# Expert gates added into a zeroed DRAM table by indirect DMAs, U remainders moved from GpSimd to VectorE

## The chip, the core and the metric

The program runs on one core of one Trainium2 chip. The metric is the device time of one execution in microseconds (us); lower is better. In the profile PE is TensorE (matmuls; PEld its weight loads), DVE is VectorE, ACT is ScalarE, POOL is GpSimd, and SP is the queue that issues the plain DMAs.

## What is computed

One decoder layer over 512 tokens of width 1024. The first half (projections, sliding-window attention and an RWKV recurrence, output projection, layer norm) is not touched but for one addition. The second half is PEER, a retrieval over 128 x 128 = 16384 single-neuron experts with rows U (1024) and V (1024):

```python
def _peer(h, wq, subkeys, U, V):
    q = (hf @ wq).reshape(T, PEER_HEADS, 2, PEER_HALF)
    s = jnp.einsum('thcd,hcnd->thcn', q, subkeys).astype(jnp.float32)
    sv, si = lax.top_k(s, PEER_TOPK)
    cand = sv[:, :, 0, :, None] + sv[:, :, 1, None, :]
    cidx = si[:, :, 0, :, None] * PEER_NKEYS + si[:, :, 1, None, :]
    fv, fpos = lax.top_k(cand.reshape(T, PEER_HEADS, PEER_TOPK * PEER_TOPK), PEER_TOPK)
    fidx = jnp.take_along_axis(cidx.reshape(T, PEER_HEADS, PEER_TOPK * PEER_TOPK), fpos, axis=-1)
    gates = jax.nn.softmax(fv, axis=-1).astype(h.dtype)
    def chunk(args):
        xc, ic, gc = args
        u = jnp.take(U, ic, axis=0)
        act = jax.nn.gelu(jnp.einsum('chkd,cd->chk', u, xc), approximate=False)
        vv = jnp.take(V, ic, axis=0)
        return jnp.einsum('chk,chkd->cd', gc * act, vv)
```

So each of 512 tokens picks 8 heads x 16 experts, and its output is the sum of gate x gelu(U row . h) x V row.

## The kernel before

The kernel has four blocks with barriers between them: projections (to about 367 us), mixing (to about 600), output projection and layer norm (to about 680), and `emit_experts`, to which all that follows belongs.

**Two ways for the tokens.** Tokens 0 to 383 (three tiles of 128, TD = 384) are computed densely: gelu(U h) for all 16384 experts is made, stored to the DRAM table `scored`, read back, multiplied by a table of gates that is zero for all but the picked experts, and multiplied by V. The last 128 tokens are computed sparsely: one indirect DMA (a gather) fetches, for pick number k of all 128 tokens, 128 rows of U (512 KB), another 128 rows of V. There are 128 picks, so 256 gathers, all issued by GpSimd (`Picked.fetch`, L1373). VectorE makes a dot product per U gather (`dot`, L1380) and a weighted sum per V gather (`add`, L1399); each is one SCALAR_TENSOR_TENSOR with both inputs in SBUF.

**The U stage.** 128 slabs of 128 experts, four to a group, so 32 groups i with slots s = 0 to 3. For every slab TensorE transposes the U rows in two halves into PSUM banks 2 and 3 (`turn`, L1295, 8 matmuls), ScalarE rounds the halves to fp32r into `uh` (`evacuate`, L1323), something subtracts to get the remainder `ul`, and TensorE makes 24 matmuls (`product`, L1315: uh with hh, uh with hl, ul with hh). On TensorE `turn` of the next slab stands ahead of `product` of this one. `turn` may write banks 2 and 3 only when the previous slab has been read out of them (`bank_out`). In groups 0 to 9 ScalarE copies the banks a second time, to `uraw` (L1330), which frees them, and GpSimd subtracts from there (`remainder`, L1338). From group 10 on VectorE subtracts out of PSUM, which frees them (`late_remainder`, L1346).

**Routing.** Groups 0 to 7 each hold one routing head: on TensorE 16 + 16 matmuls of 512 columns for the queries (L1641), then the scores (L1653) around slot 0; ScalarE hands the scores over in `SS`; VectorE finds the 16 best of 128, twice, then the 16 best of 256 sums and their expert numbers (L1854 to L1877), one head behind TensorE. Its order within a head is written out by hand.

**Gates.** After group 9 VectorE makes the softmax of all heads at once (L1884 to L1899), TensorE transposes expert numbers and gates (L1670) and ScalarE copies them out. In groups 10 to 25 (16 turns, `BLOCKS`) 96 steps spread the gates over all experts: VectorE makes one-hot matrices (`hot_step`, L1905 and L1910), TensorE multiplies them (4 matmuls a step, L1687), ScalarE copies them to `stage` (L1786), SP stores 1.5 MB a group to the table `gates` (L1535). In the same turns GpSimd fetches the picks of three columns (3 U and 3 V gathers a turn), in groups 26 to 30 of four; the rest comes in the V stage. A gather of turn t + 1 waits for the dot or the add of turn t that frees its buffer (`fetched`, L1604). TensorE and VectorE go through the groups in lockstep: DVE makes the remainders, the dots in slots 0 and 1, the adds in slots 2 and 3, in program order.

**The V stage.** 32 groups: SP loads V rows, stored scores and gates (L1538 to L1548), VectorE multiplies scores by gates and makes remainders, TensorE makes 72 matmuls a group (L1704 to L1706). Layer norm and output follow.

## Time and profile before

| what | value |
|---|---|
| time, median of 3 runs | 2102.42 us (2101.3 to 2102.5) |
| the profiled execution, its own time | 2104.01 us |
| its span, first to last instruction | 2102.3 us |
| mean granted TensorE clock | 0.964 of full |
| TensorE busy | 1918.7 us (91%) |
| VectorE busy | 1428.1 us (68%) |
| ScalarE busy | 734.1 us (35%) |
| GpSimd busy | 550.0 us (26%) |
| U stage with routing, groups 0 to 9 | about 686 to 1016 us |
| U stage, groups 10 to 25 | about 1022 to 1433 us |
| U stage, groups 26 to 31 | about 1433 to 1560 us |
| V stage | about 1560 to 2085 us |

An engine that is busy most of the time is not by that the bound: a stage is bound by the engine that never waits in it. The busy time of a matmul counts from its issue to its modelled end, and the next one is issued before that; so times of TensorE are best read as distances between start times. Times in the rows are from the start of the span.

### The profile page before, as it was taken

What the parts mean: (1) busy time and instruction counts of PE and PEld (TensorE: products, weight loads), DVE (VectorE), ACT (ScalarE), POOL (GpSimd) and SP (SyncE); (2) the same over time, 40 slices, a digit from 0 to 9 for tenths busy, and PEclk for the clock granted to TensorE, in tenths of its full rate; (3) what the DMA queues carried; (4) which work ended last, traced back from release to release, by engine and by line L of the source; (5) the groups of instructions that cost most, each with busy time, mean ns of one, the idle gap of its engine ahead of it and who ended that gap; (6) DMA issues with size and microseconds to landing.
All of it is one profiled execution on the core that took longest, in us unless ns stands there. A gap on an engine that the chain in (4) does not pass through costs nothing.

```text
span 2102.3 us, 33108 instructions
## 1 busy us (share of the span) xinstructions
PE 1918.7 (91%) x10322; PEld 1602.1 (76%) x10322; DVE 1428.1 (68%) x2902; ACT 734.1 (35%) x1305; POOL 550.0 (26%) x427
## 2 busy tenths in 40 slices
PE   2889896786967999999999999999989999999996
PEld 2343585685834687879999999999988888888885
DVE  4187435445244468687488888886758888888887
ACT  1221134343222343435444444443233333333331
POOL 3011332131100222223432233224513323233310
PEclk9999998998989999999999999999999999999998
DMA  7273100000051232434589889889979999999982
GB/s 262 98 233 127 41 1 1 0 0 0 0 201 42 90 126 96 132 99 133 206 294 299 298 296 301 296 301 336 389 281 414 368 347 359 355 353 348 355 316 79
DMA packets 244203, 434.82 MB, mean 207 GB/s; under 512 B 84578, under 2 KB 157636, under 8 KB 244164
## 3 DMA queue, kind: packets, MB, share of 16 engines
q1 hardware_dynamic: 207300, 300.12, 41.2%
q0 software_dynamic: 36864, 134.23, 17.5%
q8 instruction: 18, 0.29, 0.1%
q14 instruction: 21, 0.17, 0.0%
HBM read 379.77 MB, written 54.53 MB: 207 GB/s over the span
## 4 chain that ended last, share of the span: by engine, by line
PE 65%; DVE 1%; DMA 1%; issue 1%; ACT 0%; SPq 0%; ACTq 0%; DVEq 0%
PE bank L1315 25%; PE bank L1706 8%; PE bank L1704 8%; PE bank L1705 8%; PE bank L1641 5%; PE bank L1295 5%; PE bank L1687 4%; DMA urows<-in_peer_u 1%; PE bank L1653 1%; DVE n_stats L1118 0%; DVE wide L2008 0%; DVE wide L2006 0%; DVE wide L1127 0%; SPq L1539 0%; SPq L1543 0%
## 5 line engine op out<-in xcount | busy, mean ns | idle before, releaser
L1315 PE MATMUL bank<-hh,uh 128*128 128x384 f32 x1024 | 358.3, 350 | 0.0
L1315 PE MATMUL bank<-hl,uh 128*128 128x384 f32 x1024 | 344.4, 336 | 0.0
L1704 PE MATMUL bank<-vh,wh 128*128 128x512 f32 x768 | 299.4, 390 | 3.1 <-DVE wl L1967 3.1
L1706 PE MATMUL bank<-vh,wl 128*128 128x512 f32 x768 | 299.5, 390 | 0.0
L1705 PE MATMUL bank<-vl,wh 128*128 128x512 f32 x768 | 299.4, 390 | 0.0
L1373 POOL DMA_INDIRECT vsel<-in_peer_v,picks x128 | 151.7, 1185 | 413.0 <-DVE gt L1399 398.7
L1800 ACT ACTIVATE vh<-vraw 128x1024 fp32r<-128x1024 f32 x128 | 135.9, 1062 | 288.4 <-PE bank L1706 270.2
L1373 POOL DMA_INDIRECT usel<-in_peer_u,picks x108 | 147.9, 1369 | 247.9 <-DVE usel L1380 234.6
L1964 DVE TENSOR_TENSOR vl<-vraw,vh 128x1024 fp32r<-128x1024 f32 x128 | 156.6, 1223 | 81.1 <-ACT vh L1800 81.0
L1315 PE MATMUL bank<-hh,ul 128*128 128x384 f32 x1024 | 198.3, 334 | 0.0
L1315 PEld LDWEIGHTS bank<-hl,uh 128*128 128x128 f32 x1024 | 194.4, 190 | 0.0
L1315 PEld LDWEIGHTS bank<-hh,uh 128*128 128x128 f32 x1024 | 194.2, 190 | 0.0
L1315 PEld LDWEIGHTS bank<-hh,ul 128*128 128x128 f32 x1024 | 179.3, 188 | 0.0
L1399 DVE SCALAR_TENSOR_TENSOR gt<-vsel,wsel,gt 128x1024 f32<-128x1024 f32 x128 | 164.1, 1282 | 12.7 <-DMA vsel<-in_peer_v,picks 5.2
L1704 PEld LDWEIGHTS bank<-vh,wh 128*128 128x128 f32 x768 | 144.6, 188 | 33.5 <-DVE vl L1964 3.5
L1346 DVE TENSOR_TENSOR ul<-bank,uh 128x512 fp32r<-128x512 f32 x174 | 112.0, 685 | 84.0 <-ACT uh L1323 84.0
L1705 PEld LDWEIGHTS bank<-vl,wh 128*128 128x128 f32 x768 | 144.6, 188 | 30.0
L1706 PEld LDWEIGHTS bank<-vh,wl 128*128 128x128 f32 x768 | 144.5, 188 | 30.0
L1338 POOL TENSOR_TENSOR ul<-uraw,uh 128x1024 fp32r<-128x1024 f32 x41 | 100.5, 2452 | 234.4 <-ACT uraw L1330 234.4
L464 PE MATMUL bank<-hT,wt 128*128 128x512 f32 x320 | 147.5, 619 | 9.9 <-DMA wt<-in_w_in 5.7
L1323 ACT ACTIVATE uh<-bank 128x512 fp32r<-128x512 f32 x256 | 145.1, 606 | 12.9 <-PE bank L1295 12.5
L1295 PE MATMUL bank<-ident,urows 128*128 128x128 f32 x1024 | 135.8, 276 | 13.0 <-DMA urows<-in_peer_u 6.4
(314 smaller groups left out, 3096.3 us busy)
## 6 DMA issues: line engine op xcount, KB each, us to landing
urows<-in_peer_u SPq DMA_DIRECT2D x128, 512.0 KB
vraw<-in_peer_v SPq DMA_DIRECT2D x128, 512.0 KB
ada<-in_ada_w SPq DMA_DIRECT2D x12, 2048.0 KB
scored<-act_out SPq DMA_DIRECT2D x128, 192.0 KB
gates<-SS SPq DMA_DIRECT2D x16, 1536.0 KB
gtile<-gates SPq DMA_DIRECT2D x32, 768.0 KB
act_in<-scored SPq DMA_DIRECT2D x128, 192.0 KB
wt<-in_w_in SPq DMA_DIRECT2D x19, 512.0 KB
```

The lines of the kernel that those rows point to most:

```text
L464: last = pe.matmul(banks[slot][:, :], wt[slot][:, k, :], hT[:, k, :], start=(k == 0), stop=(k == KD - 1))
L1295: last = pe.transpose(self.banks[2 + h][:, k * P:(k + 1) * P], self.u[s][:, (4 * h + k) * P:(4 * h + k + 1) * P], self.ident[:, :])
L1315: last = pe.matmul(bank, u[:, k, :], h[:, k, :], start=(n == 0), stop=(n == 3 * KD - 1))
L1323: act.activation(self.uh[s % 2][:, 4 * h:4 * h + 4, :], self.banks[2 + h][:, :].rearrange("p (k e) -> p k e", k=4), ACT.Copy)\
L1346: dve.tensor_tensor(self.ul[s % 2][:, 4 * h:4 * h + 4, :], self.banks[2 + h][:, :].rearrange("p (k e) -> p k e", k=4), self.uh[s % 2][:, 4 ...
L1373: pool.indirect_dma_start(out=into[:, :], out_offset=None, in_=row, in_offset=bass.IndirectOffsetOnAxis(ap=self.picks[:, at:at + 1], axis=0))\
L1399: dve.scalar_tensor_tensor(out=self.y[:, :], in0=self.vsel[k][:, :], scalar=self.wsel[:, k:k + 1], in1=self.y[:, :], op0=ALU.mult, op1=ALU ...
L1704: pe.matmul(b, wh[s][:, cols], vh[s][:, half], start=first, stop=False)
L1705: pe.matmul(b, wh[s][:, cols], vl[s][:, half], start=False, stop=False)
L1706: last = pe.matmul(b, wl[s][:, cols], vh[s][:, half], start=False, stop=stop)
L1800: act.activation(vh[s][:, :], vraw[s][:, :], ACT.Copy).then_inc(vh_up, 1)
L1964: dve.tensor_tensor(vl[s][:, :], vraw[s][:, :], vh[s][:, :].bitcast(F32), ALU.subtract)\
```

## The change

Four things, as the code says it:

1. The table `gates` gets the layout [expert row 128][128][384 tokens] and is filled with zeros in the mixing block, by 16 DMAs of SP that copy the zero block of `vtok` (1.5 MB each).
2. The spreading by one-hot matrices goes, with its transposes, copies and stores. In its place GpSimd issues 384 indirect DMAs ("puts"), one per head (8), pick (16) and dense tile (3); each adds 128 gates of 4 bytes into the table, at addresses that VectorE computes per head (`places`). The puts of heads 0 to 3 (192) are issued before the first gather; then 10 follow the gathers of each of the turns of groups 10 to 25 and 8 those of each later turn. The first put of a head waits for the places and gates of the head and for the landing of the head before. SP waits for all puts before it loads gates.
3. The remainders of groups 0 to 9 move from GpSimd to VectorE, out of PSUM; ScalarE's second copy goes. In a routing head they stand at four fixed places between VectorE's top-16 instructions.
4. The softmax is made per head (`share`, four small instructions), two heads later; ScalarE's exponential as well.

The core of the diff:

```diff
+            for j in range(16):
+                sp.dma_start(flat[:, 24 * j:24 * j + 24, :], vtok[:, 0:1, :].broadcast_to([P, 24, P]))\
+                    .then_inc(cleared, 16)
+            sp.wait_ge(cleared, START + 16 * 16)
...
     def evacuate(self, act, i, s):
             act.activation(self.uh[s % 2][:, 4 * h:4 * h + 4, :],
                            self.banks[2 + h][:, :].rearrange("p (k e) -> p k e", k=4), ACT.Copy)\
                 .then_inc(self.uh_up, 1)
-            act.activation(self.uraw[:, 4 * h:4 * h + 4, :],
-                           self.banks[2 + h][:, :].rearrange("p (k e) -> p k e", k=4), ACT.Copy)\
-                .then_inc(self.bank_out, 1)
-
-    def remainder(self, pool, i, s):
-        pool.tensor_tensor(self.ul[s % 2][:, :, :], self.uraw[:, :, :], self.uh[s % 2][:, :, :].bitcast(F32),
-                           ALU.subtract).then_inc(self.ul_up, 1)
-
-    def late_remainder(self, dve, i, s):
+
+    def remainder(self, dve, i, s):
...
         # gpsimd
-            with pool.Fori(0, SPREAD) as i:
-                for s in range(4):
-                    scores.remainder(pool, i, s)
-            scores.remainder(pool, SPREAD, 0)
+            def put_gates(n):
+                for h, k, t in islice(places_of, n):
+                    if k == 0 and t == 0:
+                        pool.wait_ge(picks_up, START + 2 * h + 2)
+                        pool.wait_ge(gate_up, START + 2 * h + 5)
+                        if h:
+                            pool.wait_ge(put[h - 1], 16 * (NT - 1) * TOPK)
+                    at = (h * TOPK + k) * (NT - 1) + t
+                    pool.indirect_dma_start(out=grid, out_offset=bass.IndirectOffsetOnAxis(
+                        ap=places[:, at:at + 1], axis=0), in_=FV[:, t, h + 2, k:k + 1], in_offset=None,
+                        compute_op=ALU.add).then_inc(put[h], 16)
+            put_gates(192)
...
-            for i in range(BLOCKS):
+            for i in range(TURNS):
                 fetched(0, 3, 3 * i, 3)
+                put_gates(10)
             for i in range(LAST - CLEAR):
                 fetched(0, 4, LATER + 4 * i, 3 if i == 0 else 4)
+                put_gates(8)
...
         # vector, one routing head
-                    best16([st[:, u, :] for u in range(8)], [st2[:, u, :] for u in range(8)], sv, si, 8)
+                    share(step, h)
+                    spare = [st2[:, u, :] for u in range(8)]
+                    first8([st[:, u, :] for u in range(8)], spare, sv, si, 8)
+                    scores.remainder(dve, h, 2)
+                    second8(spare, sv, si, 8)
+                    scores.remainder(dve, h, 3)
...
-                    best16(flat[0], flat[1], fv, fp, NT)
-                    dve.tensor_copy(FV[:, :, bass.ds(h, 1), :].rearrange("p t o k -> p t (o k)"), fv[:, :, :])
+                    first8(flat[0], flat[1], fv, fp, NT)
+                    second8(flat[1], fv, fp, NT)
+                    scores.remainder(dve, h + 1, 0)
...
+                    dve.scalar_tensor_tensor(
+                        out=places[:, bass.ds(h * (NT - 1) * TOPK, (NT - 1) * TOPK)]
+                        .rearrange("p (k t) -> p t k", t=NT - 1), in0=ids[:, :, :], scalar=float(TD),
+                        in1=tokens[:, :].unsqueeze(2).broadcast_to([P, NT - 1, TOPK]), op0=ALU.mult, op1=ALU.add)\
+                        .then_inc(picks_up, 1)
                     dve.sem_inc(picked, 1)
+                    scores.remainder(dve, h + 1, 1)
...
             with dve.Fori(SPREAD, CLEAR) as i:
                 for s in range(4):
-                    for q in steps_of(s):
-                        hot_step(i, q)
                     following(i, s)
```

VectorE in the program of before, at the start of a routing head (SS are the scores, st2 the scores with the 8 best removed, gatepost a tiny copy that stands behind a wait):

```order
L1857 COPY gatepost<-iota 128x1
L1841 MAX sv<-SS 128x8 x8
L76 ISA
L1836 COPY gatepost<-iota 128x1
L1844 MAX_INDEX si<-sv,SS 128x8 x8
L1846 MATCH_REPLACE st2<-sv,SS 128x128 x8
L76 REGISTER_ALU
L1836 COPY gatepost<-iota 128x1
L1849 MAX sv<-st2 128x8 x8
```

VectorE in the changed program, at the same place; lines 1783 to 1790 are `share`, line 1334 is the remainder of slot 2 in two halves:

```order
L1785 TENSOR_REDUCE tot<-FV 128x4
L75 ISA
L1786 RECIPROCAL tot<-tot 128x4
L75 REGISTER_ALU
L1787 TENSOR_TENSOR FV<-FV,tot 128x3x16
L1790 ISA
L1790 TENSOR_TENSOR shares<-FV,tot 128x16
L1806 MAX sv<-SS 128x8 x8
...
L1811 MATCH_REPLACE st2<-sv,SS 128x128 x8
...
L1334 TENSOR_TENSOR ul0<-bank,uh0 128x512
L1333 REGISTER_ALU
L1334 TENSOR_TENSOR ul0<-bank,uh0 128x512
L1817 MAX sv<-st2 128x8 x8
```

The remainder of slot 2 now stands on VectorE behind `share` and behind the first half of the search, where before it stood on GpSimd alone.

GpSimd before, from the last remainders of groups 0 to 9 to the first gathers:

```order
L1338 TENSOR_TENSOR ul<-uraw,uh 128x1024
L1599 REGISTER_ALU
L1599 COMPARE_AND_BRANCH
L1338 TENSOR_TENSOR ul<-uraw,uh 128x1024
L1373 DMA usel<-in_peer_u,picks 128x1024 x3
L1373 DMA vsel<-in_peer_v,picks 128x1024 x3
```

GpSimd in the changed program, at the end of the 192 puts and in the first two turns (line 1577 is the put, line 1361 the gather):

```order
L1577 DMA gates<-FV,places 6291456x1 [waits mix_qks_2,exp_up_1,z_used_1]
L1577 DMA gates<-FV,places 6291456x1 x47
L1361 DMA usel<-in_peer_u,picks 128x1024 [waits z_used_1]
L1361 DMA usel<-in_peer_u,picks 128x1024 x2
L1361 DMA vsel<-in_peer_v,picks 128x1024 x3
L1577 DMA gates<-FV,places 6291456x1 [waits mix_sc_2,exp_up_1,z_used_1]
L1577 DMA gates<-FV,places 6291456x1 x9
L1361 DMA usel<-in_peer_u,picks 128x1024 [waits h_up_1] x3
L1361 DMA vsel<-in_peer_v,picks 128x1024 [waits proj_mixed_1] x3
L1577 DMA gates<-FV,places 6291456x1 x10
```

A turn of GpSimd in groups 10 to 25 was six gathers and is now six gathers and ten puts, in this order on the one queue.

## Rows read from the trace of the kernel before

**Rows 1.** Table by stretch: length, busy of each engine, clock, DMA share, GB/s.
```profile
370.00:605.00 235.00, 175.56 (x1383) 159.54 (x1382) 103.15 (x140) 87.14 (x169) 41.71 (x37) 0.90 0.01 2
688.00:976.00 288.00, 288.00 (x1427) 225.26 (x1426) 204.69 (x915) 119.79 (x224) 77.74 (x32) 1.00 0.35 112
1050.00:1420.00 370.00, 370.00 (x2558) 370.00 (x2557) 322.02 (x703) 151.74 (x289) 112.92 (x89) 1.00 0.90 297
1560.00:2080.00 520.00, 516.90 (x2277) 427.98 (x2276) 419.48 (x595) 191.78 (x282) 143.20 (x112) 1.00 0.92 338
```

**Rows 2.** Timeline of PE: start, us, line, out<-in; slot 3 in heads 2 and 3.
```profile
785.61 1.03 PE L1295 MATMUL bank<-ident,urows 128*128 128x128 f32 x8
...
821.57 1.03 PE L1295 MATMUL bank<-ident,urows 128*128 128x128 f32 x8
```

**Rows 3.** Timeline of DVE, end of routing head 2 and start of head 3.
```profile
792.44 0.22 DVE L1859 CAST sif<-si 128x128 f32<-128x128 uint32 x1
...
802.06 0.20 DVE L1864 COPY FV<-fv 128x64 f32 x1
...
808.84 1.21 DVE L1410 TENSOR_REDUCE JS<-st 128x1024 f32 x1
818.20 0.15 DVE L1857 COPY gatepost<-iota 128x1 f32<-128x1 f32 x1 [8.16 <-ACT SS L1760]
...
824.37 1.64 DVE L1849 MAX8 sv<-st 128x8 f32<-128x128 f32 x8
```

**Rows 4.** Groups by line, DVE in 1050 to 1420: busy, mean ns, idle before.
```profile
L1346 DVE TENSOR_TENSOR ul<-bank,uh 128x512 fp32r<-128x512 f32 x116 | 74.6, 684 | 45.6 <-ACT uh L1323 45.6
```

**Rows 5.** Timeline of PE at the hand-over to group 10 and in group 26.
```profile
1015.91 0.49 PE L1670 MATMUL bank<-ident,IS 128*128 128x128 f32 x3
...
1020.52 0.52 PE L1670 MATMUL bank<-ident,FV 128*128 128x128 f32 x3 [3.79 <-DVE FV L1896]
1021.89 1.97 PE L1295 MATMUL bank<-ident,urows 128*128 128x128 f32 x8 [0.85 <-issue]
...
1432.61 1.04 PE L1295 MATMUL bank<-ident,urows 128*128 128x128 f32 x8
1437.65 1.03 PE L1295 MATMUL bank<-ident,urows 128*128 128x128 f32 x8
```

**Rows 6.** Table by stretch behind that hand-over; the clock is third from the end.
```profile
1023.00:1027.00 4.00, 4.00 (x16) 4.00 (x15) 4.00 (x12) 1.20 (x2) 0.79 (x1) 0.50 1.03 416
1029.00:1031.00 2.00, 2.00 (x15) 2.00 (x14) 1.74 (x7) 0.35 (x1) 1.70 (x2) 1.00 0.44 111
```

**Rows 7.** Groups by line in 1449 to 1470, all of POOL, then three of DVE.
```profile
L1373 POOL DMA_INDIRECT usel<-in_peer_u,picks x6 | 7.7, 1282 | 1.8 <-issue 1.8
L1373 POOL DMA_INDIRECT vsel<-in_peer_v,picks x6 | 7.0, 1171 | 8.5 <-DVE gt L1399 7.2 <-issue 1.2
L1373 POOL DMA_INDIRECT uraw<-in_peer_u,picks x2 | 1.9, 940 | 0.6 <-issue 0.6
L1399 DVE SCALAR_TENSOR_TENSOR gt<-vsel,wsel,gt 128x1024 f32<-128x1024 f32 x5 | 6.4, 1284 | 5.0 <-DMA vsel<-in_peer_v,picks 4.9
...
L1380 DVE SCALAR_TENSOR_TENSOR usel<-usel,htok 128x1024 f32<-128x1024 f32 x3 | 3.7, 1222 | 2.0 <-DMA usel<-in_peer_u,picks 1.7 <-issue 0.3
L1380 DVE SCALAR_TENSOR_TENSOR uraw<-uraw,htok 128x1024 f32<-128x1024 f32 x1 | 1.2, 1226 | 0.5 <-DMA uraw<-in_peer_u,picks 0.5
```

**Rows 8.** Timeline of POOL and of DVE: gathers back to back, one landing.
```profile
1457.25 0.94 POOL L1373 DMA_INDIRECT vsel<-in_peer_v,picks  x1 [0.30 <-issue]
1458.49 1.92 POOL L1373 DMA_INDIRECT vsel<-in_peer_v,picks  x1 [0.30 <-issue]
...
1458.38 1.21 DVE L1380 SCALAR_TENSOR_TENSOR usel<-usel,htok 128x1024 f32<-128x1024 f32 x1
...
1437.01 1.68 POOL L1373 DMA_INDIRECT uraw<-in_peer_u,picks  x1 [17.53 <-DVE usel L1380]
...
1443.61 1.23 DVE L1380 SCALAR_TENSOR_TENSOR uraw<-uraw,htok 128x1024 f32<-128x1024 f32 x1 [2.25 <-DMA uraw<-in_peer_u,picks]
```

More of the change, by code:

```diff
@@ L3 @@
 from contextlib import ExitStack
+from itertools import islice
 import math
@@ L1409, in emit_pick @@
     for work, dst in ((cand, IS), (cand2, JS)):
-        last = dve.tensor_reduce(dst[:, :, bass.ds(h, 1), :].rearrange("p t o k -> p t (o k)"),
-                                 work[:, :, :, :], AX.X, ALU.add)
+        last = dve.tensor_reduce(dst[:, :, :], work[:, :, :, :], AX.X, ALU.add)
     step(last)
@@ L1457, in emit_experts @@
         act_in = sb("act_in", [P, 4, TD])
-        gt = [sb(f"gtile{q}", [P, BLOCKS, 4, TB]) for q in range(2)]
+        gt = [sb(f"gtile{q}", [P, 4, TD]) for q in range(2)]
         w = [sb(f"w{b}", [P, TD]) for b in range(2)]
@@ L1524, in _ @@
                 scores.store(sp, i, 3)
-            with sp.Fori(ROUTED, SPREAD) as i:
-                for s in range(4):
-                    experts(i, s)
-                scores.store(sp, i, 3)
-            with sp.Fori(0, BLOCKS // 2) as b:
-                for o in range(2):
-                    i = 2 * b + (SPREAD + o)
-                    for s in range(4):
-                        experts(i, s)
-                    sp.wait_ge(staged, START + 2 * STEPS * b + STEPS * (o + 1))
-                    sp.dma_start(gates[:, :, bass.ds(2 * b + o, 1), :].rearrange("p g o n -> p g (o n)"),
-                                 stage[o].rearrange("p (g j) t -> p g (j t)", j=4)).then_inc(sent[o], 16)
-                    scores.store(sp, i, 3)
             def load_v(s, g):
@@ L1555, in _ @@
                 sp.wait_ge(sk_in[c], START + 16 * HEADS)
-                sp.wait_ge(sent[c], START + 16 * (BLOCKS // 2))
+            for h in range(HEADS):
+                sp.wait_ge(put[h], 16 * (NT - 1) * TOPK)
             load_gates(0, 0)
@@ L1696, in _ @@
                     following(LAST, s)
-                scores.product(pe, LAST, s, True)
+                scores.product(pe, LAST, s)
             def tokens(s, t, first, stop):
@@ L1825, in _, with share @@
         def _(dve):
-            per = 14
+            per = 17
             chain = Tally(p_dve)
-            dve.wait_ge(iota_up, START + 1)
+            for k in range(2):
+                dve.memset(FV[:, :, k, :], 0.0).then_inc(less_up, 1)
+            dve.wait_ge(iota_up, START + 2)
+            def share(step, h):
+                top = FV[:, :, bass.ds(h, 1), :].rearrange("p t o k -> p t (o k)")
+                dve.wait_ge(exp_up, START + h + 1)
+                dve.wait_ge(gate_up, START + 2 * h)
+                step(dve.tensor_reduce(tot[:, :], top, AX.X, ALU.add))
+                step(dve.reciprocal(tot[:, :], tot[:, :]))
+                dve.tensor_tensor(top[:, 0:NT - 1], top[:, 0:NT - 1],
+                                  tot[:, 0:NT - 1].unsqueeze(2).broadcast_to([P, NT - 1, TOPK]), ALU.mult)\
+                    .then_inc(gate_up, 1)
+                dve.tensor_tensor(shares[:, bass.ds(TOPK * h, TOPK)], top[:, NT - 1],
+                                  tot[:, NT - 1:NT].broadcast_to([P, TOPK]), ALU.mult).then_inc(gate_up, 1)
+            scores.remainder(dve, 0, 0)
+            scores.remainder(dve, 0, 1)
             with dve.Fori(0, HEADS // 2) as g:
@@ L1914, in following @@
+            scores.remainder(dve, ROUTED, 2)
+            scores.remainder(dve, ROUTED, 3)
+            scores.remainder(dve, ROUTED + 1, 0)
+            share(soft, HEADS)
+            for s in range(1, 4):
+                scores.remainder(dve, ROUTED + 1, s)
+            share(soft, HEADS + 1)
+            scores.remainder(dve, SPREAD, 0)
+            dve.wait_ge(gate_up, START + 2 * (2 + HEADS))
             def following(i, s):
                 if s < 3:
-                    scores.late_remainder(dve, i, s + 1)
+                    scores.remainder(dve, i, s + 1)
@@ L1917, in following @@
                 else:
-                    scores.late_remainder(dve, i + 1, 0)
+                    scores.remainder(dve, i + 1, 0)
             with dve.Fori(SPREAD, CLEAR) as i:
@@ L1937, in _ @@
                 t = i - CLEAR
[L1938 removed]
+                turns = [t + TURNS] * 3 + [t]
                 for s in range(4):
```

251 lines of the change are left out of this document (89 added, 162 removed).

## The prediction

> **What bounds the kernel now.** I read the table by stretch first, to see in which stage which engine never rests. In the routing heads, in groups 10 to 25 and in the V stage TensorE is busy for the whole stretch or nearly, while VectorE has 83 of 288 us, 48 of 370 and 100 of 520 left and GpSimd far more [rows 1]. So every stage is TensorE's, and a change can pay only by taking work from TensorE; it can cost by making TensorE wait. The timeline of TensorE then gives the rhythm: a routing head takes 821.57 - 785.61 = 35.96 us [rows 2]; a slab 1437.65 - 1432.61 = 5.04 us, so a group without routing or spreading 20.16 us [rows 5]; a group with spreading (1432.61 - 1021.89) / 16 = 25.67 us [rows 5]. The timelines of VectorE and GpSimd show how long what stands in their queues takes [rows 3, 7, 8].
>
> **The sum, made against the profiled execution's own 2104.0 us.**
>
> *Spreading goes: -85.1.* Groups 10 to 25 took 410.7 us [rows 5]. About 3.0 of these are the half clock of their first 6 us (0.50 of full [rows 6]), which belongs to the hand-over below. Sixteen groups of 20.16 are 322.6. 410.7 - 3.0 - 322.6 = 85.1. VectorE also loses its one-hots and ScalarE its copies; neither was the bound. The 1.5 MB store per group goes too, and with it DMA share [rows 1].
>
> *Old hand-over goes: -9.0.* From the last product of group 9 (1015.9) to the first transpose of group 10 (1021.89) pass 6.0 us, for the transposes of the picks and a wait of 3.79 for the softmax [rows 5]; then the clock stands at 0.50 until between 1027 and 1029 [rows 6], which loses 3.0 more.
>
> *Remainders on VectorE in the routing heads: +37.6.* TensorE may transpose slot 3 only when slot 2's remainder has been read out of the bank. That instruction now stands behind the first half of the top-16 search. VectorE starts a head at 818.20 and reaches the second half at 824.37 [rows 3], so 6.17 us; ahead come four small instructions of the softmax, some 0.8 us (a small copy takes 0.20 [rows 3]); behind comes half a remainder, 0.68 [rows 4]. 818.20 + 0.8 + 6.17 + 0.68 = 825.9, but TensorE wants to go on at 821.57 [rows 2]: a stall of 4.3 us. The two halves of the remainder follow at 0.6 us instead of 0.4 for the transposes, here and once more at slot 3, so 4.7 a head, times 8. The start of VectorE hangs on TensorE's scores, so the stall comes back in each head. The other three remainders come in time: VectorE's head, 25 us of search and some 9 us added, still fits into 40.7.
>
> *New hand-over from head 7 to group 8: +10.8.* Group 8 has no query matmuls (14 us in a head), but VectorE is still in head 7. Counted from the freeing of slot 3: TensorE is back for group 8 after 10.3 us (two slabs and what the halves add). VectorE needs 0.6 + 4.1 (second half of the search) + 1.3 (remainder) + 9.6 (cast to the copy into FV, 792.44 to 802.06 [rows 3]) + 0.7 = 16.3: a stall of 6.0. The next remainder stands behind 8.0 us of picks (802.06 to 810.05 [rows 3]) and 0.7 of addresses, TensorE has 5.2: another 4.8.
>
> *Clock: +18.* After the idle of 3.79 us TensorE ran at half clock for about 6 us, 3 us lost [rows 5, 6]. The trace shows no stall that comes back every 40 us. The two hand-over stalls are longer than 3.79: 6 us. The eight head stalls (4.3) are just as long as the one in the rows; I take half of them, 12 us. Ends: 0 and 30.
>
> *Groups 10 to 29 become GpSimd's: +46.6.* A put appears nowhere in the trace. The nearest row is a gather, also one index per partition and 128 pieces: 0.94 us and a gap of 0.30 or 0.31, so 1.25 [rows 8]. A turn has six gathers and ten puts, in groups 26 to 29 eight and eight: 16 x 1.25 = 20.0 us. But a gather that is issued while VectorE runs an instruction with two SBUF inputs takes longer: 1.92 us beside the dot at 1458.38, 0.94 us just before it [rows 8]. In 1449 to 1470 14 gathers took 16.6 us instead of 13.2, beside 9 dots and adds [rows 7]: 0.38 each. So a turn costs GpSimd 20.0 + 6 x 0.38 = 22.3 us, later 23.0, against TensorE's 20.16. That is 16 x 2.14 + 4 x 2.84 = 45.6. Off goes what GpSimd may be late: after the last add of a turn it issues one V gather, ten puts and two U gathers (18.1 us), these land 4.9 us later (1438.69 to 1443.61 [rows 8]), 2.9 us into the turn that needs them, and VectorE can wait until 8.2 us into it before TensorE misses the remainder of slot 2: 5 us, once. On go three waits at a head's border within the turns for the landing of the last put, 0 to 4.9 us each, taken as 2. In all 45.6 - 5 + 6 = 46.6. The first 192 puts do not count: they run from about 793 us (head 0's softmax is made in head 2), take 240 us and some 20 of hold-ups and waits, and end near 1053, before group 10 starts (1015.9 + 37.6 + 10.8 + 18 = 1082).
>
> *At nothing:* the zero fill, 25.2 MB in 512-byte rows while the DMA engines are idle for 235 us [rows 1]; it needs 107 GB/s, and 297 were moved among 384-byte rows in groups 10 to 25 [rows 1]. If it came only at 100 GB/s, it would cost 17. The loads of gates in four pieces of 1536 bytes instead of one of 6144: TensorE is at 516.9 of 520 with a DMA share of 0.92 [rows 1], so 0 to 10. ScalarE's and SP's changes take work off. SP's wait for all puts: the last is issued in group 29, one group ahead of it.
>
> Sum: -85.1 - 9.0 + 37.6 + 10.8 + 18 + 46.6 = +18.9, so 2122.9 for an execution like the profiled one. That stood 1.6 over the median of the runs, so 2121 us.
>
> **Where a page speaks otherwise.** The rows show gathers held up beside two-input instructions. The Trainium skill, "SBUF — State Buffer", section "Who interferes with whom", says that such a VectorE instruction contends only with GpSimd instructions that read SBUF, and infers that generating descriptors needs the write interface and so is not stalled by it. By that inference a turn would take GpSimd 20.0 us and TensorE would stay the bound, the first rival below; the 1.92 us row speaks against it for gathers.
>
> **Rivals.**
> 1. *TensorE stays the bound.* GpSimd has 16 x 1.25 = 20.0 against 20.16 us if nothing holds it up, and a put of 4 bytes a piece may be cheaper than a gather of 4 KB rows. Then +46.6 falls away: 2104.0 - 27.7 - 1.6 = 2075 us, from 2057 (no clock loss) to 2087 (all of it). For it: 20.0 is so near 20.16 that 0.15 us less per put suffices. Against: rows 7. Chance 0.29.
> 2. *Dear puts* (slower still). An add in DRAM reads before it writes, and nothing in the trace has a price for it, on GpSimd or in the queue that the gathers share. Upper end: the longest gather shown, 1.92 + 0.30 = 2.2. At 1.6 a put, near the mean U gather of 1.28 + 0.30 [rows 7], 192 puts in the turns cost 67 us more, and the first 192 end at 1120, so group 10 is 37 late: 2225 us. At 2.2 it would be 2455. It decides from about 1.4 us a put. Chance 0.17.
> 3. *The parts cancel:* the head stalls are there, the hold-ups half as large and the clock stays up: within 4 us of 2102. Chance 0.07.
> 4. The forecast, from 2095 to 2155: 0.47.
>
> **How the numbers follow.** 2121 is the time of the likeliest case. Below 2068 lies a third of rival 1, above 2215 half of rival 2: 0.1 and 0.1. The range 2068 to 2215 holds the rest. A measurement tells this kernel from no change at about 0.2%, 4 us: faster 0.30 (rival 1 and an edge of the forecast), same 0.08, slower 0.62. The likeliest case alone would have 2095 to 2155.
>
> **What would show it.** In the profile after: matmuls of slot 3 in each head with an idle of 4.3 us behind a remainder of VectorE, and a head of 40.7 us; two waits of 5 to 6 us at group 8; GpSimd with no idle in groups 12 to 29, its DMAs 1.25 us apart with 1.6 to 2.2 beside dots and adds; VectorE's dots waiting for the U gathers; groups of 22 to 23 us. It is wrong if groups 10 to 25 come at 20.2 us (rival 1), if puts last longer than gathers or land ever later (rival 2), or if TensorE passes slot 3 without a wait.

## The result, and the profile after

| what | before | after |
|---|---|---|
| time, median | 2101.86 us (4 runs, 2099.1 to 2102.5) | 2328.94 us (4 runs, 2327.28 to 2334.11) |
| ratio, 95% interval | | 1.109 (1.107 to 1.111) |
| profiled execution, own time and span | 2104.01, 2102.3 | 2328.41, 2326.7 |
| mean granted TensorE clock | 0.964 | 0.90 |

The change costs 227 us. The forecast was 2121 with a range to 2215: its sign was right, its size and its range were wrong.

The price that the trace of before did not have comes first. The answer on the tile `gates` on GpSimd (duration in ns: least, median, most), of the profile after:

```profile
L1577 POOL DMA_INDIRECT gates<-FV,places x384: 1538/1547/2636, 796.9 to 1730.2; - x192
...
DMA to landing us min/median/max: 2.9/3.0/5.4
```

And the timeline of POOL in group 19, where puts and gathers alternate on one queue; it answers to [rows 8]:

```profile
1443.33 1.54 POOL L1577 DMA_INDIRECT gates<-FV,places  x1 [0.30 <-issue]
1445.18 0.99 POOL L1361 DMA_INDIRECT usel<-in_peer_u,picks  x1 [0.30 <-issue]
1446.48 0.96 POOL L1361 DMA_INDIRECT usel<-in_peer_u,picks  x1 [0.30 <-issue]
...
1451.46 1.00 POOL L1361 DMA_INDIRECT vsel<-in_peer_v,picks  x1 [0.30 <-issue]
1452.77 2.53 POOL L1577 DMA_INDIRECT gates<-FV,places  x1 [0.31 <-issue]
1455.60 2.00 POOL L1577 DMA_INDIRECT gates<-FV,places  x1 [0.30 <-issue]
1457.91 1.54 POOL L1577 DMA_INDIRECT gates<-FV,places  x1 [0.30 <-issue]
```

A put takes 1.54 us and a gap of 0.30, so 1.85 us from one to the next; a gather, in the same turn, still 0.94 to 1.0. The price lies in issuing: the put lands 3.0 us after its issue, sooner than the gathers of rows in the same trace (6.7 and 7.0 us, medians).

TensorE's timeline, the transposes L1303 of slot 3, which the prediction watched (they answer to [rows 2, 5]; the number in brackets is the idle time before them):

```profile
717.61 1.97 PE L1303 MATMUL bank<-ident,urows 128*128 128x128 f32 x8 [4.47 <-DVE ul L1334]
...
760.81 1.97 PE L1303 MATMUL bank<-ident,urows 128*128 128x128 f32 x8 [4.43 <-DVE ul L1334]
...
1033.15 1.63 PE L1303 MATMUL bank<-ident,urows 128*128 128x128 f32 x8 [4.38 <-DVE ul L1334]
...
1043.40 1.63 PE L1303 MATMUL bank<-ident,urows 128*128 128x128 f32 x8 [3.23 <-DVE ul L1334]
...
1174.44 1.97 PE L1303 MATMUL bank<-ident,urows 128*128 128x128 f32 x8 [83.65 <-DVE ul L1334]
...
1203.11 1.97 PE L1303 MATMUL bank<-ident,urows 128*128 128x128 f32 x8 [6.91 <-DVE ul L1334]
...
1742.40 1.97 PE L1303 MATMUL bank<-ident,urows 128*128 128x128 f32 x8 [7.34 <-DVE ul L1334]
1759.73 1.96 PE L1303 MATMUL bank<-ident,urows 128*128 128x128 f32 x8 [9.78 <-DMA urows<-in_peer_u]
```

Three things are to be seen. The head stalls are there, as forecast. At 1174 TensorE has waited 83.65 us, once, which the prediction did not have. And from there the same place comes 20 times in 1742.40 - 1174.44 = 568 us, 28.4 us a group, where it had been 20.16 without spreading or puts, and 22.3 (later 23.0) by the forecast. The releaser named is VectorE's remainder each time; what holds VectorE is one step further back, in the table of waits (us in all, times, longest):

```profile
DVE usel L1368 <- DMA usel<-in_peer_u,picks: 299.4, 37, 87.6
...
PE bank L1303 <- DVE ul L1334: 245.5, 31, 83.7
...
POOL gates L1577 <- DVE shares L1790: 116.5, 1, 116.5
```

VectorE's dots stand before the remainders in its order and wait for U gathers, and the gathers stand behind the puts on GpSimd. GpSimd itself waits little: 15.0 us in all for the landing of a head's last put (six times), 6.0 for a dot and an add between 1180 and 1650, and 116.5 once, before the first put. The table by stretch (columns as in [rows 1]) shows GpSimd at 80% in the turns and TensorE's clock down; the last line is the V stage, which did not change:

```profile
806.00:1015.00 209.00, 188.63 (x879) 148.12 (x878) 163.84 (x647) 56.17 (x103) 172.13 (x109) 0.94 0.50 98
1060.00:1140.00 80.00, 30.79 (x195) 30.27 (x193) 7.13 (x15) 12.29 (x22) 65.01 (x43) 0.72 0.40 63
1180.00:1650.00 470.00, 377.10 (x2150) 369.94 (x2149) 209.10 (x297) 105.83 (x218) 376.20 (x267) 0.87 0.73 214
1790.00:2300.00 510.00, 506.91 (x2230) 419.13 (x2229) 414.60 (x589) 190.96 (x281) 144.46 (x112) 1.00 0.94 343
```

Of the missing fifth of GpSimd's time, 94 us, 80 are gaps of 0.30 us, one before each of the 267 instructions; the other 14 are the 6.0 just named and 8.2 of the 15.0. The page's chain of work says the same in one line:

```profile
POOL gates L1577 26%; PE bank L1658 7%; PE bank L1660 7%; PE bank L1659 7%; POOL vsel L1361 3%; POOL usel L1361 2%; PE bank L1318 2%; PE bank L1620 2%; DMA gates<-FV,places 1%; DMA urows<-in_peer_u 1%; PE bank L1303 1%; DMA usel<-in_peer_u,picks 0%; DMA vsel<-in_peer_v,picks 0%; PE bank L1632 0%; DVE si L1809 0%
```

### The profile page after: what moved, and what is told of

It reads as the page before. It is cut to its first block, busy times and chain, and to the rows that moved or that the text cites. A ratio compares the mean times of both kernels' runs of the same rounds, so it can differ in the third digit from the quotient of the medians.

```text
span 2326.7 us, 30375 instructions
## 1 busy us (share of the span) xinstructions
PE 1897.5 (82%) x9545; PEld 1570.7 (68%) x9545; DVE 1336.0 (57%) x2563; ACT 632.5 (27%) x1120; POOL 1047.5 (45%) x771
## 3 DMA queue, kind: packets, MB, share of 16 engines
q0 software_dynamic: 92160, 134.46, 21.8%
## 4 chain that ended last, share of the span: by engine, by line
POOL 32%; PE 27%; issue 7%; DMA 3%; DVE 2%; ACT 0%; SPq 0%; DVEq 0%; ACTq 0%; POOLq 0%
POOL gates L1577 26%; PE bank L1658 7%; PE bank L1660 7%; PE bank L1659 7%; POOL vsel L1361 3%; POOL usel L1361 2%; PE bank L1318 2%; PE bank L1620 2%; DMA gates<-FV,places 1%; DMA urows<-in_peer_u 1%; PE bank L1303 1%; DMA usel<-in_peer_u,picks 0%; DMA vsel<-in_peer_v,picks 0%; PE bank L1632 0%; DVE si L1809 0%
## 5 line engine op out<-in xcount | busy, mean ns | idle before, releaser
L1577 POOL DMA_INDIRECT gates<-FV,places x384 | 629.4, 1639 | 246.5 <-DVE shares L1790 116.5
L1318 PE MATMUL bank<-hh,uh 128*128 128x384 f32 x1024 | 382.3, 373 | 0.0
L1303 PE MATMUL bank<-ident,urows 128*128 128x128 f32 x1024 | 162.6, 311 | 260.6 <-DVE ul L1334 245.5
L1318 PE MATMUL bank<-hl,uh 128*128 128x384 f32 x1024 | 366.0, 357 | 0.0
L1368 DVE SCALAR_TENSOR_TENSOR usel<-usel,htok 128x1024 f32<-128x1024 f32 x128 | 154.1, 1223 | 299.7 <-DMA usel<-in_peer_u,picks 299.4
L1303 PEld LDWEIGHTS bank<-ident,urows 128*128 128x128 f32 x1024 | 139.3, 161 | 276.6 <-DVE ul L1334 255.7
L1334 DVE TENSOR_TENSOR ul<-bank,uh 128x512 fp32r<-128x512 f32 x256 | 166.6, 686 | 168.5 <-ACT uh L1325 165.5
L1318 PEld LDWEIGHTS bank<-hh,uh 128*128 128x128 f32 x1024 | 215.2, 210 | 0.0
L1318 PEld LDWEIGHTS bank<-hl,uh 128*128 128x128 f32 x1024 | 213.2, 208 | 0.0
L1342 ACT ACTIVATE act_out<-bank 128x384 f32<-128x384 f32 x128 | 62.9, 491 | 438.8 <-PE bank L1318 438.7
```

Source lines behind the costliest of these rows:

```text
L1303: last = pe.transpose(self.banks[2 + h][:, k * P:(k + 1) * P], self.u[s][:, (4 * h + k) * P:(4 * h + k + 1) * P], self.ident[:, :])
L1318: last = pe.matmul(bank, u[:, k, :], h[:, k, :], start=(n == 0), stop=(n == 3 * KD - 1))
L1334: dve.tensor_tensor(self.ul[s % 2][:, 4 * h:4 * h + 4, :], self.banks[2 + h][:, :].rearrange("p (k e) -> p k e", k=4), self.uh[s % 2][:, 4 ...
L1368: dve.scalar_tensor_tensor(out=self.usel[k][:, :], in0=self.usel[k][:, :], scalar=1.0, in1=self.htok[:, :], op0=ALU.mult, op1=ALU.mult, ac ...
L1577: pool.indirect_dma_start(out=grid, out_offset=bass.IndirectOffsetOnAxis(ap=places[:, at:at + 1], axis=0), in_=FV[:, t, h + 2, k:k + 1], i ...
```

## The experiments

The theory after the result: a put costs GpSimd 1.85 us; this alone makes the two surprises (group 10 late, 28.4 us a group), and the rest of the sum holds. Rivals: the queue or DRAM is slowed by the adds and so the gathers land late; or VectorE's new work, the zero table and its loads cost as well. Runs 1 to 6 leave out some of the result (each expectation says what), so they are probes and no versions to use. Runs 2 to 7 are one execution each; executions of one kernel differ by some microseconds (2327.3 to 2334.1 for the changed one), and so only larger differences between them count.

### 1. The add taken off

```diff
-                        compute_op=ALU.add).then_inc(put[h], 16)
+                        ).then_inc(put[h], 16)
```

> The 384 puts write instead of adding (left out: the sum where two heads pick the same expert for the same token). Theory A: the add is what makes a put last 1.54 us on GpSimd where a gather lasts 0.94. Then puts fall to 0.94 and 0.30 of gap, the first 192 end before group 10 starts, groups 10 to 29 take 22 to 23 us, and the time is near the 2121 of the forecast. Theory B: writing to DRAM, or pieces of 4 bytes, makes it so. Then puts stay at 1.54 and the time at 2329.

Measured: 2121.98 us, ratio 1.009 (1.007 to 1.012); profiled 2120.6. All 384 puts are still there, with the same addresses and the same bytes (134.46 MB on GpSimd's queue either way).

```profile
L1577 POOL DMA_INDIRECT gates<-FV,places x384: 953/958/2036, 791.9 to 1523.1; - x192
```

Without the add a put costs what a gather does, 0.958 us; group 10 starts without a wait, and the first in the turns comes at 1167, of 1.2 us. The forecast had priced a put like a gather, at 1.25 us with its gap, and came out at 2121. Here the premise is true, and its parts come out too: the first 192 puts take 258 us (forecast 260), and from slot 3 of group 10 to slot 3 of group 30 pass 450.7 us (1085.35 to 1536.00, forecast 449.8). That the total agrees within 1 us is in part luck: this execution is 5 us ahead of the changed kernel's at slot 3 of head 0 (712.53 against 717.61), where the two programs do the same, and it loses 4.6 us from slot 3 of group 30 to the end (582.9 us, 578.3 in the kernel before).

So the one word `add` is worth 207 us. 384 times 0.59 us would be 227; GpSimd waits 28 us for VectorE in this run between 1050 and 1536, time that the dearer puts fill. Do the adds slow the gathers? They land 6.7 and 7.0 us after their issue with the adds and 7.1 and 8.1 without (medians, U and V rows), so this rival is out.

One more thing changes with the add, in the pages' lines on GpSimd's queue (packets, MB, share of the DMA engines), for the changed kernel, this run and run 5, which has no puts:

```profile
q0 software_dynamic: 92160, 134.46, 21.8%
q0 software_dynamic: 49152, 134.46, 17.3%
q0 software_dynamic: 36864, 134.23, 18.0%
```

The last line is 256 gathers of 144 packets each. The 384 puts add 55296, again 144 each; without the add they are 12288, 32 each. The number of packets does not set GpSimd's price by itself, since a gather of rows has 144 of them at 0.94 us.

### 2. Half the pieces

```diff
-   ap=places[:, at:at + 1], axis=0), in_=FV[:, t, h + 2, k:k + 1], in_offset=None,
+   ap=places[0:64, at:at + 1], axis=0), in_=FV[0:64, t, h + 2, k:k + 1], in_offset=None,
```

> Every put takes 64 partitions instead of 128 (left out: half the gates). If GpSimd's time for a put goes with the number of pieces, it falls from 1.54 to about 0.8 to 1.0 us and the time to 2090 to 2130; if it is a fixed cost of the instruction, it stays at 1.54 and the time at 2329.

Measured: 2289.98 us.

```profile
L1577 POOL DMA_INDIRECT gates<-FV,places x384: 1401/1410/2500, 795.3 to 1692.9; - x192
```

Half of the pieces save 0.14 us of 1.55, so neither expectation holds: it is mostly a cost of the instruction, but not all. By these two points 1.27 us hang on the instruction and 0.28 on its 128 pieces (an estimate, a straight line). Fewer pieces in each instruction save little; whether more would pay, no run shows. Nor is there a run at 64 pieces without the add, so how the add's own 0.59 us splits stays open.

### 3. Gathers of 4 bytes in place of the puts

```diff
-   pool.indirect_dma_start(out=grid, out_offset=bass.IndirectOffsetOnAxis(
-       ap=places[:, at:at + 1], axis=0), in_=FV[:, t, h + 2, k:k + 1], in_offset=None,
-       compute_op=ALU.add).then_inc(put[h], 16)
+   pool.indirect_dma_start(out=back[:, at:at + 1], out_offset=None, in_=grid,
+       in_offset=bass.IndirectOffsetOnAxis(ap=places[:, at:at + 1], axis=0)).then_inc(put[h], 16)
```

> Every put is turned round: it gathers 128 values of 4 bytes from the same addresses of the table into SBUF (left out: all gates, the table stays zero). Theory A (the add costs): 0.94 us, as the gathers of 4 KB rows, and a time near 2120. If 4-byte pieces cost GpSimd more than 4 KB rows: over 1.3 us and over 2200.

Measured: 2120.66 us.

```profile
L1578 POOL DMA_INDIRECT back<-gates,places x384: 940/944/1984, 797.6 to 1522.9; - x192
```

The same time as without the add, to 2 us. Neither the direction nor the size of the pieces (4 bytes here, 4 KB in a gather of rows) makes a difference of more than 0.02 us on GpSimd (0.944, 0.94, and 0.958 for the write); the add does.

### 4. The first 192 puts alone

The calls `put_gates(10)` and `put_gates(8)` in the turns go, and SP waits for four heads.

> The first 192 puts stay, the 192 in the turns go (left out: the gates of heads 4 to 7). My account: groups 10 to 29 fall from 28.4 to 20.2 us, 20 times 8.2 = 164 us, and the wait of 84 us at group 10 stays: about 2165. If the transfers of the puts, and not GpSimd's queue, held the groups up, or if another engine bounds them, they stay above 21 us.

Measured: 2163.2 us. The stall at group 10 is there unchanged, 84.0 of the 127.2 us in the table of waits; the other ten are the head stalls and the hand-over, 43.2 us, as in run 5. The turns run at TensorE's pace (table by stretch):

```profile
PE bank L1303 <- DVE ul L1334: 127.2, 11, 84.0
```

```profile
1180.00:1480.00 300.00, 300.00 (x1895) 298.05 (x1895) 183.89 (x266) 90.37 (x191) 108.56 (x90) 1.00 0.83 298
```

This splits the loss. The puts of the turns cost 165 us (2328.4 - 2163.2), of which the forecast had 46.6, so 118.6 too few. The first 192 cost 88 us, 2163.2 - 2075.1 of the next run, of which it had nothing. They stand ahead of the first gather only by this kernel's order; with some of them behind it, the split would be another, which no run tried.

### 5. No put at all

> The kernel after without any put; the dense tokens' gates stay zero, so their expert outputs are left out. Theory (only the puts were mis-sized, everything else in the sum holds): GpSimd has 6 gathers a turn, TensorE stays the bound in groups 10 to 31 at 20.2 us a group, routing heads still stall 4.4 us each at slot 3 and the time is 2104.0 - 27.7 - 1.6 = 2075, within 10. Rival (VectorE's new work in the turns or the zero table also costs): over 2095, with groups of more than 20.5 us though no put is there.

Measured: 2075.07 us, which was forecast as 2075 by the first rival's sum. With it all other terms stand tested together: the spreading taken off, the head stalls, the hand-over, the clock, the remainders on VectorE, the zero fill and the new loads of gates. The largest also stands by itself: groups 10 to 25 take 323.3 us (1080.29 to 1403.55) where they took 410.7, and the forecast had 322.6. So VectorE's work in the turns costs TensorE nothing. The timeline of TensorE has the head stalls as after:

```profile
760.79 1.97 PE L1303 MATMUL bank<-ident,urows 128*128 128x128 f32 x8 [4.43 <-DVE ul L1334]
```

### 6 and 7. The remainders placed earlier in a head, without puts and with them

```diff
+                    scores.remainder(dve, h, 2)
-                    first8([st[:, u, :] for u in range(8)], spare, sv, si, 8)
-                    scores.remainder(dve, h, 2)
+                    first8([st[:, u, :] for u in range(8)], spare, sv, si, 8,
+                           lambda: scores.remainder(dve, h, 3))
                     second8(spare, sv, si, 8)
-                    scores.remainder(dve, h, 3)
...
+                    scores.remainder(dve, h + 1, 0)
                     flat = [[m[:, t, :, :].rearrange
...
-                    scores.remainder(dve, h + 1, 0)
```

(The lambda runs between `max_index` and `match_replace`.)

> As the run before it in this call (no puts, the dense tokens' gates left out), and in the routing heads VectorE makes the remainder of slot 2 before the first half of the search, that of slot 3 inside it, that of the next head's slot 0 before the last search. Theory (the head stalls are made by the order on VectorE, not by its load): the idle of 4.4 us at slot 3 is gone, the clock stays at full, a head takes 36.0 to 36.5 us instead of 42.6, and the time is 50 us under the run before, about 2025. Rival (VectorE is full in a head, or another remainder is late in place of that of slot 3): a head of 39 us or more, gain under 30 us.

> The kernel after with all 384 puts, and VectorE's remainders in the routing heads placed earlier, as in the run before it in this call. Theory (from the first put on GpSimd is the bound, 384 puts of 1.85 us and its gathers in a row): the heads save 50 us, but only what comes before the first put counts, two heads of 6.6 us, so about 2315; the wait of TensorE for the first dots at group 10 grows from 84 to about 120 us. Rival (the head stalls and the puts add up): 2329 - 50 = 2279.

Measured: 2030.48 us without puts, 45 less than run 5, and 2320.67 with all puts, 8 less than after. The timeline of TensorE of run 6, slot 3 of heads 0 and 1 (compare 717.61 and 760.81 above):

```profile
717.66 1.03 PE L1303 MATMUL bank<-ident,urows 128*128 128x128 f32 x8
...
753.80 1.04 PE L1303 MATMUL bank<-ident,urows 128*128 128x128 f32 x8
```

This head takes 36.1 us again, without idle time and at full clock, and so do the others (35.9 to 37.0, two of them with idle of 0.3 and 0.7 us): the stalls came from the place of an instruction on VectorE, not from its load. The gain is 5 us under the expectation; the hand-over to group 8 now has waits of 2.1 and 11.3 us, where run 5 had 4.4 and 3.0. In run 7, expected at 2315, the same 45 us are worth 8, since GpSimd is the bound from the first put (785.1 instead of 796.9) to the last. The wait for it only grows, from 83.7 to 118.3 (table of waits):

```profile
PE bank L1303 <- DVE ul L1334: 259.4, 25, 118.3
```

### 8 to 11. A version that uses what is free

What the runs say together: GpSimd had time in the turns of before (113 of 370 us busy, [rows 1]). With a third of the spreading gone a turn would be 23.7 us, of which the gathers take GpSimd 9.8; at 1.85 us the rest holds seven puts and no more. So: two of the three dense tiles spread by one-hot matrices as before (4 steps a turn, not 6), the third put, by 128 puts into a table of its own. Remainders and softmax stay as before. The core of run 8 against the kernel before:

```diff
-TB = TD // BLOCKS
+TS = 2 * P
+TB = TS // BLOCKS
...
+                    pool.indirect_dma_start(out=grid, out_offset=bass.IndirectOffsetOnAxis(
+                        ap=places[:, at:at + 1], axis=0), in_=FV[:, 2, h, k:k + 1], in_offset=None,
+                        compute_op=ALU.add).then_inc(put[h], 16)
...
                 fetched(0, 3, 3 * i, 3)
+                put_gates(7)
```

> The kernel before, in which only two of the three dense tiles are spread by one-hot matrices (4 steps a turn in place of 6) and the third is put by 128 adding DMAs into a zeroed table of its own, 7 in each turn of groups 10 to 25 and 3 or 4 in each of the next five; remainders and softmax as before. Theory (a put costs GpSimd 1.85 us, a gather 1.25 and 0.38 per dot or add beside it): GpSimd needs 6 x 1.25 + 2.3 + 7 x 1.85 = 22.8 us a turn, under TensorE's 20.16 + 85.1 / 16 x 2 / 3 = 23.7, in the later turns 23.9 against 20.2, five times but late only once the slack of 16 turns is used up. So a third of the spreading goes, 28 us: about 2074, ratio 0.987, at most 15 us more for the later turns. Rival (the puts cost TensorE time by themselves, through DMA or VectorE, whoever is the bound): over 2095, no gain.

Measured: 2097.79 us, ratio 0.998 (0.997 to 0.999), where about 2074 was expected. The slabs are shorter as expected, 5.92 us where nothing waits (1104.73 to 1110.65), but most of it is lost again: 8.7 us in groups 10 to 25, which take 391.0 instead of 382.3, and 13.5 from group 26 on, mostly in two places. Timeline of TensorE, then of GpSimd, then of SP, all of run 8:

```profile
1447.19 1.97 PE L1308 MATMUL bank<-ident,urows 128*128 128x128 f32 x8 [5.35 <-DVE ul L1359]
...
1528.35 1.97 PE L1308 MATMUL bank<-ident,urows 128*128 128x128 f32 x8 [12.46 <-DMA urows<-in_peer_u]
```

```profile
1427.52 0.94 POOL L1386 DMA_INDIRECT vsel<-in_peer_v,picks  x1 [5.34 <-DVE gt L1412]
1428.76 1.61 POOL L1635 DMA_INDIRECT third<-FV,places  x1 [0.30 <-issue]
1430.67 2.35 POOL L1635 DMA_INDIRECT third<-FV,places  x1 [0.30 <-issue]
1433.33 1.56 POOL L1635 DMA_INDIRECT third<-FV,places  x1 [0.30 <-issue]
1435.19 1.56 POOL L1635 DMA_INDIRECT third<-FV,places  x1 [0.30 <-issue]
1437.05 1.00 POOL L1386 DMA_INDIRECT usel<-in_peer_u,picks  x1 [0.30 <-issue]
```

```profile
1496.38 5.42 SPq L1299 DMA_DIRECT2D scored<-act_out  x2
1512.32 0.35 SPq L1567 DMA_DIRECT2D gtile<-gates  x1
...
1517.37 0.90 SPq L1294 DMA_DIRECT2D urows<-in_peer_u  x2
```

GpSimd waits 5.3 us for an add, and only then does it issue its puts, ahead of the U gathers that VectorE needs next; the 8 us of puts lie on the path though there was time for them before. And SP stands from 1502 to 1512 in the wait for the last put (issued at 1509), with loads of U rows queued behind it. GpSimd also waited 33.3 us in all at six borders between heads, for the landing of the put before. So run 9 issues the same puts in half turns, behind the U gathers and behind the V gathers, none after group 29; run 10 puts the last 16 all behind U gathers; run 11 also changes SP:

```diff
             for s in range(4):
+                experts(LAST - 1, s)
                 sp.wait_ge(scores.a_sent[s], START + 16)
                 load_act(s, 0)
                 load_v(s, 0)
-            for s in range(4):
-                experts(LAST - 1, s)
```

> The kernel of the run before (two tiles spread, the third put), with the same 128 puts in half turns: 4, or 3 where GpSimd needs room, behind the U gathers and as many behind the V gathers, so that a head's last put has landed by the next head's first; none after group 29. Theory (that run lost its gain in the order on GpSimd: a bunch of 4 to 7 puts between the last add and the next U gathers, which cost stalls of 5.4 us at 1447 and hold-ups of 2 us in four turns, and in SP's wait for puts issued until 1509, which cost 12.5 us at 1529): the stalls of TensorE in groups 10 to 31 are gone or under 2 us in all, groups 10 to 25 take 23.7 us each, and the time is 2075 to 2080, ratio about 0.988. Rival (the DMA engines are full, 0.97 of them in groups 10 to 25 of that run, and stalls come from there): waits for urows or gathers stay, 2090 or more.

> The kernel of the run before; the last head's 16 puts stand four at a time behind the U gathers of turns 26 to 29, none behind the V gathers of turns 25 to 29. Theory (what stands between the last add of a turn and the next turn's U gathers is on TensorE's path there, also two puts of 1.9 us): the idle of 5.4 us at 1442 and the two of 0.6 and 1.0 fall under 1 us in all and with them some 3 us of half clock; about 8 us less than the run before, 2080. Rival (turn 26 is late because it has eight gathers for six, whatever the puts): the idle stays over 3 us, gain under 3 us.

> The kernel of the run before it in this call, and SP issues the first loads of V rows and scores of the V stage one pair behind each load of U rows in group 30, not all eight ahead of them. Theory (TensorE's idle of 7.5 us at 1518, and of 6.41 us at 1535 in the kernel before, for U rows comes from these eight loads of 192 and 512 KB ahead on the same queue): that idle goes and with it some 3 us of half clock, about 10 us less than the other run of this call, 2070. Rival (the V stage then starts late instead): an equal wait appears at its start, gain under 3 us.

| run | median us | before, same chip | ratio, 95% interval |
|---|---|---|---|
| 8 | 2097.79 | 2102.34 | 0.998 (0.997 to 0.999) |
| 9 | 2088.45 | 2100.97 | 0.994 (0.992 to 0.995) |
| 10 | 2082.81 | 2100.15 | 0.992 (0.990 to 0.994) |
| 11 | 2077.59 | 2100.15 | 0.989 (0.987 to 0.991) |

Run 9 was expected at 2075 to 2080: its groups 10 to 25 were in order, but the idle of 5.4 us stayed, at 1442, behind a bunch of two puts, and 7.5 for U rows. Run 10 left 5.0 of the 7.1 us of idle that run 9 had behind VectorE's remainders, in two waits of 1.4 and 3.5 us, so its expectation (under 1 us, 8 us less in time) was missed. Its rival, that turn 26 is late because it has eight gathers for six, fits what is left, but no run shows it. In run 11 the wait for U rows is 1.4 us instead of 9.2 (timelines of TensorE, runs 10 and 11):

```profile
1514.30 1.96 PE L1308 MATMUL bank<-ident,urows 128*128 128x128 f32 x8 [9.16 <-DMA urows<-in_peer_u]
```

```profile
1511.28 1.09 PE L1308 MATMUL bank<-ident,urows 128*128 128x128 f32 x8 [1.37 <-DMA urows<-in_peer_u]
```

Run 11 was expected 10 us below run 10, and its median is 5 below. The traces show 12 us gained from group 26 to the end (668.5 against 680.6 us), but run 11's execution came to group 26 6.8 us later, by stretches in which the two kernels do the same; why, no view shows.

The wait for U rows is older than the change, since the kernel before has it with 6.41 us at 1535. Hence one more run.

### 12. SP's order alone, on the kernel before

> The kernel before with SP's new order alone (each first pair of loads of the V stage behind a load of U rows of group 30), no puts, all three tiles spread. It says how much of the best hybrid's gain (ratio 0.989) is SP's order. Theory (additive): the idle of 6.41 us at 1535 and some 2 us of half clock go, about 2093 to 2095, ratio 0.996 to 0.997; the hybrid of spreading and puts then is worth the other 0.8%. Rival (the order is worth nothing without puts, since the V stage starts late in its place): within 2 us of the kernel before.

Measured: 2094.86 us against 2101.76, ratio 0.996 (0.995 to 0.998), as expected; the wait for U rows is gone from its trace. If the two gains add up, of run 11's 1.1% about 0.35 come from SP's order and 0.8 from the mix of spreading and puts. Run 11, 2077.59 us, is the fastest kernel of this study that computes everything. With the whole third of the spreading (85.1 / 3 = 28.4 us) on top of run 12 it would be at 2066. Of the 11 us between, the two traces show 3.6 in groups 10 to 25 (385.9 instead of 382.3 us) and 7.6 from group 26 on (668.5 against 660.9), where run 11's two waits behind remainders and the wait for U rows stand.

One way was not tried: more addresses in one put. Every indirect DMA of these kernels is given one index per partition, so three tiles need three instructions.

## Why the prediction was wrong

**The step that failed** is the price of a put in "Groups 10 to 29 become GpSimd's": "A put appears nowhere in the trace. The nearest row is a gather, also one index per partition and 128 pieces: 0.94 us and a gap of 0.30 or 0.31, so 1.25". It is 1.85 (run 1 shows that the add alone makes the difference); for a put without the add the reading off the gather was right. In the turns the mechanism was right, the engine was right, the size was off by half; the size then also overturned a second step, "The first 192 puts do not count". What follows from it:

- *A turn:* forecast 22.3 and 23.0 us, measured 28.4 on average. Ten times 0.60 is 6.0 of the 6.1 us. Over 20 groups 568 instead of 449.8 us, +118.2.
- *The first 192 puts:* forecast to end near 1053, ahead of group 10. They took 369 us (192 x 1.85 = 355, the rest 7 of waits and some 7 of hold-ups) and ended at 1166; TensorE at slot 3 of group 10 was due at 1092.4 and came at 1174.44, +82.0. "They do not count" held only for a cheap put; run 4 shows this part alone.
- *From slot 3 of group 30 to the end:* 584.3 us instead of 578.3, +6.0; 3.4 of them are the wait for U rows, 9.78 us instead of 6.41.

These make 206.2 us; between 2328.4 and the 2122.9 forecast for such an execution lie 205.5.

**What held**, tested as a sum by run 5 (2075.07 measured, 2075 worked out; that it is this near is luck, since some of the parts below are off by 2 or 3 us and cancel):

- *Spreading, -85.1:* run 5's 323.3 us.
- *Zero fill and gate loads at nothing.* Slot 3 of head 0 would come at 717.61 - 4.47 = 713.1 without its stall, 713.69 in the kernel before; executions that do the same up to there scatter over 7 us (712.53 in run 1, 719.46 in run 4), so a smaller cost would not show. The V stage has 506.9 of 510 us busy [rows 1], and from its last transposes of U rows to the end pass 549.6 us, 549.5 before. But the fill did not run where the prediction put it. The first part names 367 us as the start of the mixing block; its first matmul in the trace of before is at 257. The 16 fills stand at 255 to 345 us, with the DMA engines full:

```profile
255.00:345.00 90.00, 69.55 (x530) 62.81 (x531) 41.41 (x56) 35.21 (x66) 22.47 (x21) 0.89 1.01 281
```

  TensorE is busy for 69.6 of these 90 us, 69.8 before. So 281 GB/s went by beside the mixing block at no cost that shows, where the prediction needed 107.

- *Head stalls:* forecast 4.3 us, measured 4.4. *New hand-over:* forecast two waits of 6.0 and 4.8, measured 4.4 and 3.2. The second does not follow from what the prediction names, 8.0 and 0.7 against 5.2, which leaves 3.5.
- *Clock:* forecast that half of the eight head stalls lower it. All do: each is followed by transposes of 1.97 us instead of 1.03, at a granted clock of 0.50 (here the table by stretch behind the one at 888.35, the clock third from the end; it answers to [rows 6]), and a head takes 43.2 or 42.2 us, where stall and halves make 40.7; about 2 us each, not 3 for half of them. Together with the smaller hand-over this came out even: TensorE reached group 10's second transposes at 1174.44 - 83.65 - 10.1 = 1080.7, forecast 1082.

```profile
888.00:890.00 2.00, 1.65 (x9) 1.66 (x9) 2.00 (x9) 0.50 (x1) 0.45 (x1) 0.50 0.14 0
```

- *Hold-ups of GpSimd beside VectorE's two-input instructions:* forecast 6 x 0.38 = 2.3 us a turn. In 1180 to 1650 puts took 1.67 on average, 0.13 over their median, ten a turn; with the gathers' 0.3 that is 1.6 us, and 0.5 for waits at a head's border. They fall on puts too: 2.53 and 2.00 us at 1452.77 and 1455.60, beside these two dots (timeline of VectorE):

```profile
1452.60 1.23 DVE L1368 SCALAR_TENSOR_TENSOR usel<-usel,htok 128x1024 f32<-128x1024 f32 x1 [0.93 <-DMA usel<-in_peer_u,picks]
...
1454.94 1.22 DVE L1368 SCALAR_TENSOR_TENSOR usel<-usel,htok 128x1024 f32<-128x1024 f32 x1
```

  In that window the 85 puts beside no dot and no add took 1.54 to 1.60 us, also beside a remainder; the 80 beside one took 1.81 on average, at most 2.60. So the inference of the Trainium skill, "SBUF — State Buffer", section "Who interferes with whom", that generating descriptors is not stalled is not borne out here. Whether it is the descriptors that are held up, or the reading of the put's indices out of SBUF, no run separates.
- *The slack of "5 us, once":* its 18.1 us for 13 DMAs hold more than 13 x 1.25 = 16.3, and the prediction does not say what. It moves the time by 2 us at most.

**The rivals.** *Dear puts* is what happened, with a chance of 0.17. Its line through 1.6 us (2225) and 2.2 us (2455) gives 2321 at 1.85, and 2328.9 was measured. *TensorE stays the bound* is the kernel of run 5, not this one. The range ended at 2215 because half of that case, from 2225 up, was left out above it. A price that no row shows and that is multiplied by 384 moves the time more than all other terms together; its bounds, up to 2.2 us, should have set the upper end of the range.

## What to carry to other kernels

Before work is moved to an engine as many small instructions, time one of them in exactly its form, with its compute option: on a queue with one issuer, count x price is nearly the whole answer, and an engine that was idle for two thirds becomes the bound at once. On an in-order engine the place is worth as much as the number: an instruction that nobody waits for belongs ahead of a wait that the engine has to sit through anyway, never between that wait and what the others need next (runs 6, 8 and 9). And where the bound has moved, as in run 7, repairing the old bound's stalls gives back almost nothing; 45 us became 8.

## What the runs showed of the hardware

- An indirect DMA with an add takes GpSimd 1.547 us to issue, the same without it 0.958, a gather of 128 pieces of 4 bytes 0.944, and of 4 KB 0.94. At 64 pieces the one with an add takes 1.410. What GpSimd does in the 0.59 us is open: the runs show only that it is the add's. With the add a put of 128 pieces is 144 packets on the DMA queue, as a gather of 4 KB rows is, and without it 32.
- A put with an add was held up beside VectorE's dots and adds, which read two inputs from SBUF: up to 2.60 us instead of 1.54.
- TensorE's transposes behind the idle stretch of 4.4 us took 1.97 us in all eight heads, and the granted clock there was 0.50, the lower of its two levels, 1.2 GHz. In run 6, where nothing was waited for, they took 1.03.
